# Latent-attention heads with moved gate tiles and the second rope half on GpSimd, and a second block with projection tiles on either side of the weighted sums

## The chip, the cores and the metric

One NeuronCore of a Trainium2 chip runs the whole forward pass of two blocks in one launch. The metric is the device time of that launch in microseconds (us). All engines run their own instruction streams, written out by hand, and meet in semaphores: TensorE (PE), VectorE (DVE), ScalarE (ACT), GpSimd (POOL) and the DMA queues, of which SP issues most.

## What is computed

Two blocks on a sequence of 512 positions of width 1024, in float32. The first has a pooling layer and a latent-attention layer (16 heads, 128 + 64 rope dimensions), the second a mixed layer of forgetting attention (8 heads of 64) and spatial gating, and a feed-forward. Cut to what the change touches:

```python
def mla_layer(x, cos, sin, norm_g, w_in, q_norm_g, w_q_b, kv_norm_g, w_kv_b, w_out):
    h = rmsnorm(x, norm_g)
    q_lat, kv_lat, k_rope, z = split(h @ w_in)            # z: the gates, 2048 wide
    q = (rmsnorm(q_lat, q_norm_g) @ w_q_b)                # per head 128 + 64
    kv = (rmsnorm(kv_lat, kv_norm_g) @ w_kv_b)            # per head k 128, v 128
    q_rope, k_rope = apply_rope(q_rope, cos, sin), apply_rope(k_rope, cos, sin)
    o = causal_mla_attention(q_nope, q_rope, k_nope, k_rope, v)
    return x + (o.reshape(B, S, MLA_WIDTH) * jax.nn.silu(z)) @ w_out

def second_block(x, ...):
    h = rms_norm(x, mix_norm_g) @ w_in                    # q, k, v, 8 gate logits, z
    log_f = jax.nn.log_sigmoid(f_logit + b_f)
    attn = forgetting_attention(q, k, v, log_f)
    sgu = spatial_gating(jax.nn.gelu(z), sgu_ln_g, sgu_ln_b, w_s, b_s)
    merged = concatenate([rms_norm(attn, out_norm_g[:D_ATTN]), rms_norm(sgu, out_norm_g[D_ATTN:])])
    x = x + merged @ w_out
    gate, up = split(rms_norm(x, ffn_norm_g) @ w_gate_up)
    return rms_norm(x + (silu(gate) * up) @ w_down, final_norm_g)
```

## The kernel before

Every float32 product is made of three passes with operands split in a high part (rounded to the matmul format) and the rest: high x high, high x low, low x high (`three`, L1347 to L1349). So each operand has a `_hi` and a `_lo` tensor; `_hi` is a copy by ScalarE, `_lo` a subtraction by VectorE or GpSimd.

The weights come as a stream of tiles of 128 x 1024 (512 KB). SP loads tile t into one of two `raw` buffers once the low part of tile t - 2 is made; ScalarE copies it into `w_hi` (L495, `split_tile`, three tiles ahead of its use), GpSimd subtracts into `w_lo` (L448), in a ring of four. TensorE waits for `tile_lo`, and sets `tile_used` at the tile's end. A whole tile is 24 matmuls of 512 columns (8 chunks x 3).

*Latent heads.* The projection `mla_in` makes five latent tiles, the key rope and 16 gate tiles z. Then heads come in four groups of four. For head h TensorE does: transposes of the probabilities for key blocks 0 and 1 (L1486, 7 matmuls), the scores of head h + 1 for query blocks 0 and 1 (L1347 to L1349, L1475, L1476), transposes for blocks 2 and 3 (3 matmuls), the scores for blocks 2 and 3, the weighted sum (`weigh_mla`), and then the units of the next group (`prepare`): keys, queries, two rope halves and values. The transposes of blocks 2 and 3 use the banks of blocks 0 and 1 again, so they wait until ScalarE (L655) and VectorE (L1101) have taken those out as `prob_t`. VectorE also takes the maxima (`peaks`, L1085), scales the probabilities (L1095), makes the low parts of the units (L995) and turns the rope queries: `turn_half` has two steps for half 0 (L1006, L1007) and four for half 1 (L1009 to L1014), `turned_low` two more; SP copies the turned rows into `rope_q` with 16 small DMAs a group (L391). The last group prepares nothing, so the last four heads stand directly one behind the other. The output product `mla_out` reads `y_hi` and `y_lo`, the latter made by GpSimd (L455).

*Second block.* Nine tiles `mix_qk` (four q, one with the 8 gate columns, four k), four `mix_v`, eight `mix_z`. Two z tiles are done ahead of the heads, one after each of the first six heads. A head's scores read `stacked`, into which SP copies its rows (L414, L416) while it also loads tiles. The layer norm of z's second half is on VectorE and GpSimd (L468, L470, L473). Then `sgu_mix`, the norms of both branches, and `mix_out`, in which one tile holds the weights of both branches for one output chunk; VectorE puts the two together in three steps for each chunk (L1290 to L1292), and the feed-forward's first tile starts with the last chunk of the norm (L867).

## Time and profile before

| | |
|---|---|
| time, median of 3 runs | 1397.96 us (1396.8 to 1399.28) |
| the profiled execution, own time | 1397.48 us |
| its span, first to last instruction | 1395.8 us |
| mean granted TensorE clock | 0.987 |
| busy: PE, DVE, ACT, POOL | 1340.8, 649.7, 538.4, 553.0 us |
| DMA | 135.42 MB, mean 97 GB/s |

The span is a little shorter than the time, which also holds what lies before and after the first and last instruction. A matmul's row ends later than the next one starts, since they are pipelined; starts are the better measure. The waits of an engine are sorted by the one it was released by.

### The profile page before, as it was taken

How to read it: one execution, taken by the hardware profiler on the slowest of the kernel's cores; microseconds unless marked ns; L12 is line 12 of the kernel's file. 1: busy time of each engine (PE TensorE's matmuls, PEld its weight loads, DVE VectorE, ACT ScalarE, POOL GpSimd, SP SyncE). 2: the span in 40 equal slices, each digit the busy share in tenths (PEclk: the TensorE clock that was granted, in tenths of full speed). 3: DMA queues.
4: the chain of work that ended last, by engine and by line, in shares of the span. 5: the costliest groups of instructions: out<-in, count | busy, mean ns of one | idle time of the engine just before them, and what ended most of it. 6: DMA issues, size and time to landing. Idle time of an engine off the chain costs nothing.

```text
span 1395.8 us, 16722 instructions
## 1 busy us (share of the span) xinstructions
PE 1340.8 (96%) x6170; PEld 1090.9 (78%) x6170; DVE 649.7 (47%) x1029; ACT 538.4 (39%) x893; POOL 553.0 (40%) x247
## 2 busy tenths in 40 slices
PE   7999999999999999999899999979899999999997
PEld 5888888887788777877788778877678888888886
DVE  7998547133643466565234853566642222221001
ACT  5233333233232555656533334664332322222112
POOL 4446444443353422214644443162344444444441
PEclk9999999999999999999999999998999999999999
DMA  4233322324132421322222346431222332222231
GB/s 154 88 106 119 99 91 91 106 91 150 61 121 69 143 61 46 98 54 76 91 91 97 114 151 160 107 113 55 82 91 90 96 100 90 90 95 86 92 102 64
DMA packets 40587, 135.42 MB, mean 97 GB/s; under 512 B 5936, under 2 KB 5936, under 8 KB 40016
## 3 DMA queue, kind: packets, MB, share of 16 engines
q1 hardware_dynamic: 38800, 126.18, 28.8%
q10 hardware_dynamic: 1728, 8.44, 1.6%
q8 instruction: 39, 0.64, 0.2%
q14 instruction: 20, 0.16, 0.0%
HBM read 117.76 MB, written 6.29 MB: 89 GB/s over the span
## 4 chain that ended last, share of the span: by engine, by line
PE 85%; DVE 5%; ACT 4%; issue 3%; POOL 1%; DMA 1%; SPq 0%; DVEq 0%; ACTq 0%; POOLq 0%
PE bank L1347 27%; PE bank L1349 27%; PE bank L1348 27%; PE bank L1486 1%; DVE prob_t L1101 1%; ACT f_prob L639 1%; PE bank L1476 1%; POOL w_lo L448 1%; PE bank L1475 1%; DVE pool_sqsum L877 1%; PE bank L1371 0%; DMA x<-x_in 0%; ACT w_hi L495 0%; DVE ffn_xg L867 0%; DVE y_out L1329 0%
## 5 line engine op out<-in xcount | busy, mean ns | idle before, releaser
L448 POOL TENSOR_TENSOR w_lo<-raw,w_hi 128x1024 fp32r<-128x1024 f32 x209 | 513.9, 2460 | 782.7 <-ACT w_hi L495 782.6
L495 ACT ACTIVATE w_hi<-raw 128x1024 fp32r<-128x1024 f32 x209 | 220.4, 1055 | 428.5 <-PE bank L1349 384.6
L1347 PE MATMUL bank<-ffn_xg,w_hi 128*128 128x512 f32 x352 | 141.0, 400 | 5.1 <-DVE ffn_xg L867 5.1
L1348 PE MATMUL bank<-ffn_xg,w_hi 128*128 128x512 f32 x352 | 140.2, 398 | 0.0
L1349 PE MATMUL bank<-ffn_xg,w_lo 128*128 128x512 f32 x352 | 140.2, 398 | 0.0
L1347 PE MATMUL bank<-pool_xg,w_hi 128*128 128x512 f32 x256 | 103.2, 403 | 9.2 <-DVE pool_xg L867 9.2
L1348 PE MATMUL bank<-pool_xg,w_hi 128*128 128x512 f32 x256 | 102.6, 401 | 0.0
L1349 PE MATMUL bank<-pool_xg,w_lo 128*128 128x512 f32 x256 | 102.5, 400 | 0.0
L1347 PE MATMUL bank<-y_hi,w_hi 128*128 128x512 f32 x256 | 101.5, 397 | 0.0
L1348 PE MATMUL bank<-y_lo,w_hi 128*128 128x512 f32 x256 | 101.5, 396 | 0.0
L1349 PE MATMUL bank<-y_hi,w_lo 128*128 128x512 f32 x256 | 101.5, 396 | 0.0
L1347 PEld LDWEIGHTS bank<-ffn_xg,w_hi 128*128 128x128 f32 x352 | 66.6, 189 | 22.8 <-DVE ffn_xg L867 6.5
L1349 PEld LDWEIGHTS bank<-ffn_xg,w_lo 128*128 128x128 f32 x352 | 66.7, 190 | 16.3
L1348 PEld LDWEIGHTS bank<-ffn_xg,w_hi 128*128 128x128 f32 x352 | 66.7, 190 | 16.2 <-issue 0.2
L892 DVE TENSOR_TENSOR x<-bank,x 128x512 f32<-128x512 f32 x16 | 11.1, 692 | 128.5 <-PE bank L1349 128.5
L1347 PE MATMUL bank<-w_hi,act 128*128 128x512 f32 x176 | 70.8, 403 | 0.0
L1347 PE MATMUL bank<-mla_xg,w_hi 128*128 128x512 f32 x176 | 70.6, 401 | 0.0
L1349 PE MATMUL bank<-mla_xg,w_lo 128*128 128x512 f32 x176 | 69.8, 396 | 0.0
L1348 PE MATMUL bank<-mla_xg,w_hi 128*128 128x512 f32 x176 | 69.8, 396 | 0.0
L1349 PE MATMUL bank<-w_hi,act 128*128 128x512 f32 x176 | 69.3, 394 | 0.0
L1348 PE MATMUL bank<-w_lo,act 128*128 128x512 f32 x176 | 69.0, 392 | 0.0
L1347 PEld LDWEIGHTS bank<-pool_xg,w_hi 128*128 128x128 f32 x256 | 48.9, 191 | 21.3 <-POOL w_lo L448 9.1
(327 smaller groups left out, 2815.8 us busy)
## 6 DMA issues: line engine op xcount, KB each, us to landing
raw<-stream SPq DMA_DIRECT2D x209, 512.0 KB, 3.4
spill<-x ACTq DMA_DIRECT2D x2, 2048.0 KB, 6.5
rope_q<-turned_hl SPq DMA_DIRECT2D x64, 64.0 KB, 2.5
stacked<-fq SPq DMA_DIRECT2D x24, 128.0 KB
stacked<-fk SPq DMA_DIRECT2D x24, 128.0 KB
x<-x_in SPq DMA_DIRECT2D x4, 512.0 KB, 6.6
x<-spill ACTq DMA_DIRECT2D x1, 2048.0 KB, 7.7
x<-spill SPq DMA_DIRECT2D x1, 2048.0 KB, 8.3
```

Source lines behind the costliest of these rows:

```text
L448: pool.tensor_tensor(w_lo[:, j % RING, :], raw[:, j % RAW, :], plain(w_hi[:, j % RING, :]), ALU.subtract).then_inc(tile_lo, 1)
L495: act.activation(w_hi[:, t % RING, :], raw[:, t % RAW, :], ACT.Copy).then_inc(tile_hi, 1)
L639: act.activation(target[:, ROW[b]:ROW[b + 1]], bank[SCORE_BANK[b]][:, SCORE_AT[b]:SCORE_AT[b] + n], ACT.Exp, bias=neg_peak[:, h % 2, b:b + ...
L877: dve.tensor_tensor(total, total, square(k), ALU.add).then_inc(n.summed, 1)
L892: dve.tensor_tensor(x[:, k, :], bank[(k + 4) % 8][:], x[:, k, :], ALU.add).then_inc(n.x_ready, 1)
L1101: dve.tensor_tensor(lo[:, COLUMN[b]:COLUMN[b + 1]], bank[3 + b % 2][:, 0:S - P * b], plain(hi[:, COLUMN[b]:COLUMN[b + 1]]), ALU.subtract). ...
L1347: pe.matmul(target, a_hi, b_hi, start=start, stop=False)
L1348: pe.matmul(target, a_hi, b_lo, start=False, stop=False)
L1349: return pe.matmul(target, a_lo, b_hi, start=False, stop=stop)
L1475: pe.matmul(target, rope_q[:, g % 2, j, a], rope_k_hi[:, 0:n], start=False, stop=False)
L1476: last = pe.matmul(target, rope_q[:, g % 2, j, a], rope_k_lo[:, 0:n], start=False, stop=True)
L1486: last = pe.transpose(bank[3 + b % 2][:, P * (q - b):P * (q - b + 1)], source[:, ROW[q] + P * b:ROW[q] + P * (b + 1)], ident[:])
```

## The change

In the latent layer:
- `TILE_SIZES`: the last 3 of the 16 gate tiles leave `mla_in` and become `mla_late`. The normalised input they need, `mla_xg_hi` and `mla_xg_lo`, is written to `xg_spill` by two DMAs of ScalarE's queue at the stage's start and read back by SP (`reload`, four DMAs into `zx`). TensorE does one late tile (`late_gate`) after each of heads 12, 13 and 14; ScalarE takes their silu there, and VectorE their evacuation.
- The scores of query block 2 move ahead of the second transposes. With the last head, where there are no scores, the first output tile stands in their place, four chunks at a time.
- For groups 1 to 3 ScalarE copies the bank of rope half 1 to `rope_2`, and GpSimd does its four steps and the two low parts (`turn_rows`).
- `y_lo` of chunks 8 to 15 goes from GpSimd to VectorE, after the last head. VectorE does `peaks` of bank 1 before the low parts of blocks 2 and 3.

In the second block:
- The gate tile goes; its 8 columns ride with the first z quarter, in two tiles of 1056 columns (`stream_wide`), whose four position blocks each have a bank of their own with 264 columns. The four transposes of the gates go with it.
- The tiles are in one list, `MIX`. Ahead of the heads: q0, k0, z0, z1, v0 to v3, q1, k1. The other ten stand in the heads, in `fill`: one part before the weighted sum and one after it. All scores of the next head come before the second transposes.
- `mix_out` has four tiles for the attention half and four for the gating half. `attn_product` is spread over heads 6 and 7, the gating and the norms; VectorE adds the attention half first (two steps a chunk, `add_attention`), then the gating half (one step). ScalarE, not VectorE, scales the gating branch. VectorE gates within the last head.
- The feed-forward starts with chunks 0 to 6 of its first two tiles, then chunk 7 of both (`first_tiles`).
- SP issues the stacking copies two or more tiles earlier for the last heads.

The diff, cut to its core:

```diff
-TILE_SIZES = (..., ("mla_in", LC + 1 + PC + 1),
-              ("heads", 5 * GROUPS - 1), ("mla_out", PC), ("mix_qk", 9), ("mix_v", 4), ("mix_z", 8),
+ZN = PC - 3
+TILE_SIZES = (..., ("mla_in", LC + 1 + ZN + 1),
+              ("heads", 5 * GROUPS - 1), ("mla_late", PC - ZN), ("mla_out", PC), ("mix", 20),
+MIX = (("q", 0), ("k", 0), ("z", 0), ("z", 1), ("v", 0), ("v", 1), ("v", 2), ("v", 3), ("q", 1), ("k", 1),
+       ("q", 2), ("k", 2), ("z", 2), ("z", 3), ("q", 3), ("k", 3), ("z", 4), ("z", 5), ("z", 6), ("z", 7))
...
 SP
+            sp.wait_ge(mla.scores, 3 * 12)
+            sp.wait_ge(zx_spilled, 32)
+            sp.wait_ge(rope_q_in, 256 * GROUPS)
+            for i in range(3):
+                reload(i)
+            load(0, TILE["heads"] + 5 * GROUPS + 1)
+            sp.wait_ge(tile_used, group_tile(GROUPS - 1, GH) + 1)
+            reload(3)
+            heads_after = {11: (0, 1), 13: (2, 3), 17: (4, 5), 19: (6,), 21: (7,)}
...
 POOL
+            def turn_rows(g):
+                pool.wait_ge(unit_evac, evacuated(("rope", g, 0)))
+                pool.wait_ge(rope_copied, g)
+                for i, (t, table, op) in enumerate(((turned_1, sin, ALU.subtract), (turned_2, cos, ALU.add))):
+                    pool.tensor_tensor(rope_t[:], rope_2[:], table[:], ALU.mult).then_inc(turn_steps, 1)
+                    pool.wait_ge(turn_steps, 2 * g - 1 + i)
+                    pool.tensor_tensor(t[:], t[:], rope_t[:], op).then_inc(turned, 1)
+                    pool.wait_ge(turned, 2 * g + i + 1)
+                for i, t in enumerate((turned_1, turned_2)):
+                    pool.wait_ge(turned_hi_done, 2 * g + i + 1)
+                    pool.tensor_tensor(turned_lo[:, i, :], t[:], plain(turned_hi[:, i, :]), ALU.subtract)...
...
 DVE, latent heads
                 if h + 1 < HEADS:
-                    peaks(mla, h + 1, MLA_SCALE, (0,))
+                    peaks(mla, h + 1, MLA_SCALE, (0, 1))
                 transposed_low(mla, h, prob_t_hi, prob_t_lo, (2, 3))
...
+            for k in range(8, PC):
+                dve.wait_ge(y_hi_done, PC + k + 1)
+                dve.tensor_tensor(y_lo[:, k, :], z[:, k, :], plain(y_hi[:, k, :]), ALU.subtract).then_inc(y_last_done, 1)
...
 PE, latent heads
-                for blocks in ((0, 1), (2, 3)):
+                for blocks, behind in (((0, 1), (0, 1, 2)), ((2, 3), (3,))):
                     transposes(mla, h, prob, probs, NB * (h + 1), blocks)
                     if h + 1 < HEADS:
-                        scores_mla(h + 1, blocks)
+                        scores_mla(h + 1, behind)
+                    else:
+                        pe.wait_ge(mla_evac, LC + 1 + ZN + 2)
+                        out_tile("mla_out", 0, PC, range(4) if blocks[0] == 0 else range(4, 8))
                 weigh_mla(h)
                 if g < GROUPS:
                     prepare(g, j)
+                elif h < HEADS - 1:
+                    late_gate(h - 12)
...
 PE, second block
+            def fill(h, part):
+                if h == 0:
+                    qk_tile(4 + part)
+                elif h == 2:
+                    pe.wait_ge(z_evac, NB + 2 * part + 2)
+                    qk_tile(6 + part)
+                elif h in (1, 3):
+                    sgu_tile(h + 1 + part)
+                elif h < 6:
+                    sgu_tile(h + 2, range(2 * part, 2 * part + 2))
+                elif h == 6 and part == 0:
+                    attn_product(0, (0, 1))
+                    attn_product(1, (0, 1))
             for h in range(FOX_HEADS):
+                transposes(fox, h, f_prob, probs, NB * (HEADS + h + 1), (0, 1))
+                if h + 1 < FOX_HEADS:
+                    scores_fox(h + 1, (0, 1, 2))
+                else:
+                    attn_product(0, (2,))
+                    attn_product(1, (2,))
+                    pe.wait_ge(ws_lo_done, 1)
+                    pe.wait_ge(zvn_lo_done, NB)
+                    sgu_mix(range(6))
+                transposes(fox, h, f_prob, probs, NB * (HEADS + h + 1), (2, 3))
+                fill(h, 0)
+                if h == FOX_HEADS - 1:
+                    sgu_mix((6, 7))
                 weigh_fox(h)
+                fill(h, 1)
...
 DVE, output of the second block
+            def add_attention(chunks):
+                for k in chunks:
+                    wait_half(0, k)
+                    t = mixed[:, k % 2, :]
+                    settle(dve.tensor_tensor(t, bank[ATTN_BANK[k]][:], attn_inv[:], ALU.mult))
+                    dve.tensor_tensor(x[:, k, :], t, x[:, k, :], ALU.add).then_inc(attn_added, 1)
+            add_attention(range(4))
             for c in range(SC):
+                if c == 2:
+                    add_attention((4,))
                 dve.wait_ge(sgu_hi_done, c + 1)
                 dve.scalar_tensor_tensor(sgu_lo[:, c, :], ...)
+            add_attention(range(5, DC))
...
```

How the instructions stand on the engines at three places. First TensorE in the second block, from the first transposes of a head to what follows its second transposes (`ident,f_prob` are transposes, `stacked` scores, `f_prob_t,fv` the weighted sum); before:

```order
L1486 MATMUL bank<-ident,f_prob 128x128 x7
L1613 MATMUL bank<-stacked 128x128
L1614 MATMUL bank<-stacked 128x128
L1613 MATMUL bank<-stacked 128x256
L1614 MATMUL bank<-stacked 128x256
L1486 MATMUL bank<-ident,f_prob 128x128 x3
L1613 MATMUL bank<-stacked 128x384
L1614 MATMUL bank<-stacked 128x384
L1613 MATMUL bank<-stacked 128x512
L1614 MATMUL bank<-stacked 128x512
L1347 MATMUL bank<-f_prob_t,fv 128x512
```

and the same place, head 0, in the changed kernel:

```order
L1638 MATMUL bank<-ident,f_prob 128x128 x7
L1783 MATMUL bank<-stacked 128x128
L1784 MATMUL bank<-stacked 128x128
L1783 MATMUL bank<-stacked 128x256
L1784 MATMUL bank<-stacked 128x256
L1783 MATMUL bank<-stacked 128x384
L1784 MATMUL bank<-stacked 128x384
L1783 MATMUL bank<-stacked 128x512
L1784 MATMUL bank<-stacked 128x512
L1638 MATMUL bank<-ident,f_prob 128x128 x3
L1490 MATMUL bank<-mix_xg,w_hi 128x512
```

The four longer score matmuls moved ahead of the second transposes, and a projection tile (24 matmuls, the first is shown) stands between them and the weighted sum.

Second, VectorE after the first head of a group (`turned` and `rope_t` are the rope queries, `k` a unit's low part, `prob_t` the transposed probabilities of the next head); before:

```order
L1125 TENSOR_TENSOR z<-bank,z 128x512
L995 TENSOR_TENSOR k<-bank,k 128x512
L1006 TENSOR_TENSOR turned<-bank,cos 128x512
L1007 TENSOR_TENSOR turned<-bank,sin 128x512
L1009 TENSOR_TENSOR rope_t<-bank,sin 128x512
L1010 TENSOR_TENSOR turned<-turned,rope_t 128x512
L1012 TENSOR_TENSOR rope_t<-bank,cos 128x512
L1014 TENSOR_TENSOR turned<-turned,rope_t 128x512
L1101 TENSOR_TENSOR prob_t<-bank,prob_t 128x512
```

and in the changed kernel:

```order
L1232 TENSOR_TENSOR z<-bank,z 128x512
L1098 TENSOR_TENSOR k<-bank,k 128x512
L1109 TENSOR_TENSOR turned<-bank,cos 128x512
L1110 TENSOR_TENSOR turned<-bank,sin 128x512
L1204 TENSOR_TENSOR prob_t<-bank,prob_t 128x512
```

Four steps left VectorE there. They are on GpSimd now, between weight tiles (`w_lo`), third place:

```order
L504 TENSOR_TENSOR rope_t<-rope,sin 128x512
L506 TENSOR_TENSOR turned<-turned,rope_t 128x512
L504 TENSOR_TENSOR rope_t<-rope,cos 128x512
L506 TENSOR_TENSOR turned<-turned,rope_t 128x512
L510 TENSOR_TENSOR turned_hl<-turned,turned_hl 128x512 x2
L496 TENSOR_TENSOR w_lo<-raw,w_hi 128x1024 x5
```

Before, GpSimd had nothing but `w_lo` in the heads; now six steps come in each of three groups, and the next weight tile of its stream stands behind them.

## Rows read from the trace of the kernel before

**Rows 1.** The page: its head, TensorE's line, the granted clock of 40 slices.
```profile
span 1395.8 us, 16722 instructions
...
PE 1340.8 (96%) x6170; PEld 1090.9 (78%) x6170; DVE 649.7 (47%) x1029; ACT 538.4 (39%) x893; POOL 553.0 (40%) x247
...
PEclk9999999999999999999999999998999999999999
```

**Rows 2.** Waits of TensorE: released by; us in total, times, longest.
```profile
PE bank L1486 <- DVE prob_t L1101: 11.5, 16, 2.0
...
PE bank L1486 <- DVE f_prob_t L1101: 8.2, 7, 2.0
PE bank L1347 <- DVE ffn_xg L867: 5.1, 2, 3.4
PE bank L1613 <- DMA stacked<-c_parts: 3.6, 1, 3.6
PE bank L1486 <- DVE prob L1095: 2.7, 3, 0.9
PE bank L1347 <- DVE x L1292: 2.0, 1, 2.0
PE bank L1347 <- DVE zu L1225: 1.7, 1, 1.7
```

**Rows 3.** Windows: length; busy PE, PEld, DVE, ACT, POOL; clock; DMA share, GB/s.
```profile
540.00:620.00 80.00, 75.96 (x387) 63.37 (x387) 51.17 (x129) 44.19 (x103) 16.80 (x7) 0.96 0.18 52
920.00:1020.00 100.00, 83.70 (x376) 67.96 (x375) 65.77 (x98) 46.07 (x83) 41.81 (x23) 0.88 0.28 93
```

**Rows 4.** Timeline of TensorE in `mla_in`: start, duration, instruction.
```profile
459.77 0.40 PE L1348 MATMUL bank<-mla_xg,w_hi 128*128 128x512 f32 x1
...
460.94 0.40 PE L1347 MATMUL bank<-lat,w_hi 128*128 128x512 f32 x1
```

**Rows 5.** Timeline of TensorE, first head of a group; in brackets idle before, releaser.
```profile
551.24 0.28 PE L1475 MATMUL bank<-rope_k,rope_q 128*128 128x256 f32 x1
551.36 0.28 PE L1476 MATMUL bank<-rope_k,rope_q 128*128 128x256 f32 x1
553.38 0.70 PE L1486 MATMUL bank<-ident,prob 128*128 128x128 f32 x3 [1.74 <-DVE prob_t L1101]
```

**Rows 6.** Timeline of VectorE at the same place.
```profile
552.55 1.15 DVE L1101 TENSOR_TENSOR prob_t<-bank,prob_t 128x512 fp32r<-128x512 f32 x2
```

**Rows 7.** Timeline of TensorE in a head of the second block.
```profile
884.49 0.70 PE L1486 MATMUL bank<-ident,f_prob 128*128 128x128 f32 x3 [0.78 <-DVE f_prob_t L1101]
```

**Rows 8.** Groups by line: busy us, mean ns; idle before, releaser.
```profile
L448 POOL TENSOR_TENSOR w_lo<-raw,w_hi 128x1024 fp32r<-128x1024 f32 x209 | 513.9, 2460 | 782.7 <-ACT w_hi L495 782.6
L455 POOL TENSOR_TENSOR y_lo<-z,y_hi 128x512 fp32r<-128x512 f32 x16 | 20.1, 1292 | 6.6 <-ACT y_hi L554 6.6
L495 ACT ACTIVATE w_hi<-raw 128x1024 fp32r<-128x1024 f32 x209 | 220.4, 1055 | 428.5 <-PE bank L1349 384.6 <-DMA raw<-stream 41.5 <-DVE mix_sqsum L877 2.3
```

**Rows 9.** DMA issues: KB each, us to landing; and one row of SP's timeline.
```profile
raw<-stream SPq DMA_DIRECT2D x209, 512.0 KB, 3.4
...
x<-spill SPq DMA_DIRECT2D x1, 2048.0 KB, 8.3
...
615.45 4.95 SPq L391 DMA_DIRECT2D rope_q<-turned_hl  x8
```

**Rows 10.** VectorE beside GpSimd: timeline rows, and the line's least, median and most ns.
```profile
901.01 0.88 DVE L1095 TENSOR_SCALAR f_prob<-f_prob,inv_sum 128x128 f32<-128x128 f32 x3
...
922.47 4.21 DVE L1095 TENSOR_SCALAR f_prob<-f_prob,inv_sum 128x128 f32<-128x128 f32 x3
...
972.67 2.60 DVE L1292 TENSOR_TENSOR x<-mixed,x 128x512 f32<-128x512 f32 x1
...
972.32 2.40 POOL L448 TENSOR_TENSOR w_lo<-raw,w_hi 128x1024 fp32r<-128x1024 f32 x1 [19.52 <-ACT w_hi L495]
...
L1292 DVE TENSOR_TENSOR x<-mixed,x x8: 691/2020/2691, 972.7 to 1014.6; 128x512 f32<-128x512 f32 x8
```

748 lines of the change are left out of this document (442 added, 306 removed).

## The prediction

> **What bounds the kernel now.** I read the page first, then the list of waits of TensorE, then windows, then single places of the timeline. The page shows TensorE busy for 96% of the span of 1395.8 us and its clock granted at nine tenths or more in all but one of 40 slices [rows 1]. So only two things can bring time: matmuls that go, and moments in which TensorE stands still or runs at half clock. The list of waits gives the second by cause [rows 2]. In the sixteen latent heads it is the second group of transposes behind VectorE's `prob_t` (11.5 us in 16 waits) and the first group behind `prob` (2.7 in 3). In the second block it is the same for `f_prob_t` (8.2 in 7), the copies into `stacked` (3.6), the first products of the feed-forward (5.1), the output product (2.0) and the gating (1.7). Everything ahead of the heads is not touched.
>
> A listed wait is a little short of what it costs. Two score matmuls start 0.12 us apart (551.24, 551.36), the transposes start at 553.38, 2.02 later, and the list calls 1.74 of that idle [rows 5]: the modelled tail hides 2.02 - 0.12 - 1.74 = 0.16 us of each wait. The granted clock is 0.96 over 80 us of the heads and 0.88 over the 100 us around the end of the second block's attention and its output product [rows 3]; full clock there would be worth at most 0.04 x 80 = 3.2 and 0.12 x 100 = 12 us. TensorE is busy 83.7 of those 100 us, so I count 10. In both windows the lowered level (1.2 instead of 2.4 GHz) comes with the idle places.
>
> **The change, part by part.**
>
> *The gate tile.* The ninth query/key tile, which held eight useful columns, goes: 8 chunks x 3 matmuls of 512 columns. Five such steps take 460.94 - 459.77 = 1.17 us, 0.234 each [rows 4]: 24 x 0.234 = 5.6 us, and nothing waits there, so it is all on the path. The four small transposes of the gates go too (0.3). The gates now ride as 8 more columns on two z tiles: 96 matmuls x 8 columns at 0.234/512 us a column = 0.35. Net **-5.6**.
>
> *The latent heads.* Between the two groups of transposes TensorE has now three score blocks instead of two; the third is 5 matmuls of 384 columns, 5 x 384 x 0.234/512 = 0.88 us. The waits there average 11.5/16 = 0.72, and most are shorter than 0.88. The first head of a group waits 1.74 because VectorE does the four steps of the second rope half first and reaches `prob_t` only at 552.55 [rows 5, 6]; these four, and the two low parts, go to GpSimd, with ScalarE copying the bank. The last four heads have no preparation to hide behind; three gate tiles of the first projection (3 x 5.6 us) come behind them, moved, not added, so they cost nothing in themselves and cover the 2.7 and the last four `prob_t` waits. Gain: 11.5 + 2.7 + 19 x 0.16 = 17.2, plus the clock's 3.2: 20.4.
> What it costs. (a) `y_lo` 8 to 15 now stand on VectorE behind the last head: the second output tile waits for z (0.68) and the first `y_lo` (0.69) and may meet GpSimd once (below); bounds 0.7 and 4, I take 2. (b) GpSimd's turn is four steps, then two low parts, at 1.29 each for this size [rows 8], with ScalarE's high parts between, which it reaches only in the next head: the low part is ready about as late as before, but the heads until then are shorter by their waits, and SP's 16 copies take twice 4.95 us with a tile load between [rows 9]. I get the last copy landing within half a microsecond of the scores that need it: 0 to 2 us in each of three groups, I take 1 in all. (c) Spilling and reloading the normalised input, 4 MB each way: a reload of 2 MB landed after 8.3 us [rows 9], so the 3.5 MB that stand ahead of one tile load on SP's queue take about 14.5; by the program that tile's split comes some 16 us after the reload may start and the landing some 17.5: 1 us, bounds 0 and 6. The spill has three tiles of lead (16 us) and costs nothing. Net **-16.4**.
>
> *The second block.* Projection tiles stand now before and after each weighted sum, and all score blocks before the second transposes. In the head at 882 the transposes wait 0.78 us, 0.94 with the hidden part [rows 7], with four score matmuls as cover; the other four (two of 384 and two of 512 columns) add 1792 x 0.234/512 = 0.82. With the third transpose, which waits once more for VectorE, I leave 0.35 us a head of the 8.2. The copies for the last head are issued two tiles earlier, so the 3.6 goes. The output product is cut into an attention half, which fills the gating and the norm's root, and a half that needs only one addition per chunk; the feed-forward does seven chunks of two tiles (14 x 3 x 0.234 = 9.8 us) before it needs the last chunk: 5.1 + 2.0 go. With the gating, 8.2 + 3.6 + 5.1 + 2.0 + 1.7 = 20.6, tails 12 x 0.16 = 1.9, clock 10: 32.5.
> What it costs: transposes 7 x 0.35 = 2.5; `prob` of the first head needs the fourth projection evacuated first, 0.7; the layer norm's chain on GpSimd (four blocks of two steps of 1.29, three weight tiles of 2.46, then four low parts of 1.29 [rows 8]: 12 x 1.29 + 3 x 2.46 = 23 us) against 22 us of TensorE work up to the gating's matmuls, and ScalarE held for its input before head 6: 0 to 9, I take 4.5; the last head's gating 1.5; the output product waiting for the normed branch behind the additions, 0 to 6, I take 2.5; one half-clock stretch that stays, 1.7. Together 13.4, net **-19.1**.
>
> Where GpSimd and VectorE meet decides (a) and the last block. At 972 VectorE's addition of two SBUF operands takes 2.60 us and ends with GpSimd's 2.40 us weight step, and the eight of its line range from 0.69 to 2.69; the three scalings of `f_prob`, 0.88 us together at 901, take 4.21 at 922 while GpSimd works on the layer norm [rows 10]. The Trainium skill, "SBUF — State Buffer", section "Who interferes with whom", says that a VectorE instruction with two SBUF inputs, or in a two-port mode, and a GpSimd instruction exclude each other for their whole length. By that rule the trace agrees, and the change puts more on both sides: 18 steps on GpSimd, 8 `y_lo` and 8 additions on VectorE.
>
> **Sum.** -5.6 - 16.4 - 19.1 = -41.1. The profiled execution took 1397.48 us (span 1395.8), within 0.5 us of the median of 1397.96. 1397.5 - 41.1 = **1356.4 us**.
>
> **Rivals.**
> 1. *Nearly all waits go.* The costs above are at their lower ends: of 58.5 us gained (5.6 + 20.4 + 32.5) only the transposes' 1.5, `y_lo` 0.7 and a clock stretch 1.7 stay. 1397.5 - 54.6 = 1343. For it: the fillers are 2.8 to 5.6 us long where the waits are 1 to 2. Against: the chains of the layer norm and the output product are not shortened. Chance 0.17.
> 2. *VectorE and GpSimd hold each other.* Each of the 16 two-operand steps moved onto or kept on VectorE meets a GpSimd step and takes 2.6 instead of 0.69 (+1.9) [rows 10], half of them in front of TensorE: 8 x 1.9 = 15. 1371. For it: 2.0 us is the median of those eight steps now. Against: in the heads VectorE has 3.5 to 5.6 us behind its last scaling. This is the case that the cited section would foretell. Chance 0.17.
> 3. *Slower: the weight ring runs dry.* Each of the eight heads of the second block asks for two tiles; if ScalarE reaches their splits only behind its exponentials, load 3.4 [rows 9], split 1.06 and GpSimd's 2.46 [rows 8] stand open in front of TensorE in each: 6.9 x 8 = 55 us against 41 gained: 1411. It decides from 41/8 = 5.1 us a head. For it: two raw buffers, and SP's queue holds the stacking waits between loads. Against: the ring is three tiles ahead (5.6 us each). Chance 0.03.
> 4. *The late gate tiles do not fill:* the change does not do there what it says. Their input lands late or the head-side copies hold the queue, and head 12 waits for it, 8 us more than the 1 taken: 1364. Chance 0.05.
>
> **Numbers.** The forecast has 0.58, its own range 1347 to 1365. The range to hold the time 8 times in 10 takes in the nearer parts of rivals 1 and 2 and all of 4: 1339 to 1373. A difference under 0.2% (2.8 us) could not be told from none. Faster 0.96, same 0.01, slower 0.03.
>
> **What would show it.** Right: about 24 + 4 fewer matmuls; the waits for `prob_t` and `f_prob_t` under 4 us together instead of 19.7; none for `ffn_xg`; clock 0.98 or more over the 100 us before the feed-forward; the heads from first scores to output product 3 x 5.6 - 16 us longer than before, that is about equal. Left over: waits for `zvn_lo`/`prob_t` at heads 6 and 7 of the second block, for `y_lo` once, for `sgu_lo`. Wrong: waits for w_lo on TensorE's weight loads (rival 3), for `zx` (rival 4), `y_lo`, additions and scalings on VectorE at 2 us and more with TensorE behind them (rival 2), or half-clock stretches as many as before.

## The result and the profile after

The changed kernel takes **1349.01 us** (median of 4 runs, 1346.8 to 1349.57) against 1398.62 for the kernel before in the same job: ratio 0.9637, 95% interval 0.961 to 0.9664. Forecast were 1356.4 us, with the range 1339 to 1373. The profiled execution has a span of 1347.8 us, 48.0 less than that of before. One execution of the kernel before, in the last job, took 2186.01 us at a mean granted clock of 0.557 and is left out of every comparison.

The head of the page, TensorE's line and its clock answer to [rows 1]:

```profile
span 1347.8 us, 16621 instructions
...
PE 1316.0 (98%) x6142; PEld 1075.7 (80%) x6142; DVE 647.5 (48%) x1014; ACT 540.0 (40%) x903; POOL 564.1 (42%) x256
...
PEclk9999999999999999999999999999999999999999
```

There are 28 matmuls fewer, and TensorE is busy for 98% of the span. The list of its waits answers to [rows 2]:

```profile
PE bank L1490 <- DVE pool_xg L970: 9.3, 1, 9.3
PE bank L1638 <- DVE f_prob_t L1204: 3.6, 2, 2.7
PE bank L1490 <- DVE y_lo L1243: 2.9, 2, 1.5
PE bank L1490 <- DVE attn L1326: 1.9, 1, 1.9
PE bank L1490 <- DVE v L1098: 1.8, 1, 1.8
...
PE bank L1862 <- DVE sgu L1425: 0.9, 1, 0.9
PE bank L1638 <- DVE mean_sq L1271: 0.8, 1, 0.8
PE bank L1638 <- DVE f_prob L1198: 0.5, 1, 0.5
```

All 16 waits for `prob_t` are gone, of those for `f_prob_t` two of seven are left, and `stacked` and `ffn_xg` don't appear. New are `y_lo`, `attn`, `v` and `mean_sq`. The wait at the very start (`pool_xg`, 9.3) was there before. Two windows of the changed kernel, columns as in [rows 3]: 80 us of heads at the same place of the work as there, and the last 100 us before the feed-forward:

```profile
521.70:601.70 80.00, 79.90 (x445) 68.69 (x444) 50.20 (x137) 49.41 (x118) 34.51 (x20) 1.00 0.28 86
866.00:966.00 100.00, 93.02 (x525) 79.53 (x525) 79.68 (x132) 62.14 (x119) 46.32 (x25) 0.97 0.33 106
```

The second window of [rows 3] reaches 14 us into the feed-forward. The last 100 us before it are, in the trace of before:

```profile
905.00:1005.00 100.00, 87.17 (x445) 73.65 (x444) 63.53 (x118) 51.04 (x100) 40.02 (x22) 0.91 0.25 82
```

The granted clock is 1.00 instead of 0.96 in the heads, 0.97 instead of 0.91 ahead of the feed-forward.

Where the 48.0 us went, by the first start of each stage in the two traces:

| from, to | before | after | difference | predicted |
|---|---|---|---|---|
| start, first `mla_in` matmul (no edit there) | 328.2 | 327.2 | -1.0 | 0 |
| first `mla_in` matmul, first scores | 147.0 | 129.7 | -17.3 | -16.8, moved |
| first scores, first `mix` matmul | 292.1 | 291.4 | -0.7 | +16.8 - 16.4 |
| first `mix`, first feed-forward matmul | 238.4 | 217.8 | -20.6 | } -5.6 - 19.1 |
| first feed-forward, first down projection | 256.2 | 247.7 | -8.4 | } |
| the rest | 134.0 | 134.0 | 0 | 0 |
| sum | 1395.8 | 1347.8 | -48.0 | -41.1 |

The latent part gave 18.0 for 16.4, the second block 29.0 for 24.7, and 1.0 us came from a stretch in which nothing was edited.

### The profile page after: what moved, and what is told of

The parts are those of the page before. It is cut to its first block, busy times and chain, and to the rows that moved or that the text cites. A ratio compares the mean times of both kernels' runs of the same rounds, so it can differ in the third digit from the quotient of the medians.

```text
span 1347.8 us, 16621 instructions
## 1 busy us (share of the span) xinstructions
PE 1316.0 (98%) x6142; PEld 1075.7 (80%) x6142; DVE 647.5 (48%) x1014; ACT 540.0 (40%) x903; POOL 564.1 (42%) x256
## 4 chain that ended last, share of the span: by engine, by line
PE 91%; DVE 4%; ACT 2%; DMA 1%; POOL 1%; issue 0%; DVEq 0%; SPq 0%; ACTq 0%
PE bank L1490 29%; PE bank L1492 29%; PE bank L1491 29%; PE bank L1638 2%; DMA raw<-stream 1%; PE bank L1627 1%; PE bank L1628 1%; DVE pool_xg L970 1%; PE bank L1514 1%; DVE x L1418 1%; DVE y_lo L1243 0%; DVE pool_sqsum L980 0%; DMA x<-x_in 0%; DVE y_out L1472 0%; POOL w_lo L496 0%
## 5 line engine op out<-in xcount | busy, mean ns | idle before, releaser
L496 POOL TENSOR_TENSOR w_lo<-raw,w_hi 128x1024 fp32r<-128x1024 f32 (+1 forms) x208 | 513.3, 2470 | 730.3 <-ACT w_hi L566 730.3
L566 ACT ACTIVATE w_hi<-raw 128x1024 fp32r<-128x1024 f32 (+1 forms) x208 | 218.4, 1054 | 385.7 <-PE bank L1492 322.9
L1490 PE MATMUL bank<-mla_xg,w_hi 128*128 128x512 f32 x152 | 60.9, 400 | 0.0
L1491 PE MATMUL bank<-mla_xg,w_hi 128*128 128x512 f32 x152 | 60.1, 396 | 0.0
L1492 PE MATMUL bank<-mla_xg,w_lo 128*128 128x512 f32 x152 | 60.1, 395 | 0.0
```

Source lines behind the costliest of these rows:

```text
L496: pool.tensor_tensor(w_lo[:, j % RING, 0:width], raw[:, j % RAW, 0:width], plain(w_hi[:, j % RING, 0:width]), ALU.subtract).then_inc(tile_ ...
L566: act.activation(w_hi[:, t % RING, 0:width], raw[:, t % RAW, 0:width], ACT.Copy).then_inc(tile_hi, 1)
L1490: pe.matmul(target, a_hi, b_hi, start=start, stop=False)
L1491: pe.matmul(target, a_hi, b_lo, start=False, stop=False)
L1492: return pe.matmul(target, a_lo, b_hi, start=False, stop=stop)
```

## Three places where TensorE still waits

**The transposes of head 6 of the second block.** TensorE, then ScalarE, from the timelines of the changed kernel:

```profile
899.87 0.39 PE L1784 MATMUL bank<-stacked 68*128 68x512 f32 x1
902.93 0.30 PE L1638 MATMUL bank<-ident,f_prob 128*128 128x128 f32 x1 [2.67 <-DVE f_prob_t L1204]
...
898.44 1.06 ACT L566 ACTIVATE w_hi<-raw 128x1024 fp32r<-128x1024 f32 x1 [4.20 <-DMA raw<-stream]
899.41 2.17 ACT L881 ACTIVATE zvn_hi<-zv 128x512 fp32r<-128x512 f32 x4
901.49 0.95 ACT L738 ACTIVATE f_prob_t<-bank 128x512 fp32r<-128x512 f32 x2
```

The list names VectorE, which only came last: ScalarE waited 4.2 us for a weight tile, and did the four `zvn_hi` before it took out the transposed probabilities.

The list of the weight loads' waits has one row that the matmuls' list does not show. The first of its two waits is the one at the start, the second ends at 913.21, in front of the products on `attn`; VectorE's step beside it:

```profile
PEld bank L1490 <- POOL w_lo L496: 11.4, 2, 9.3
...
910.25 2.84 DVE L1326 SCALAR_TENSOR_TENSOR attn<-attn,cols 128x512 fp32r<-128x512 f32 x1
```

GpSimd makes the four `zvn_lo` first and the weight tile's low part from 910.08 to 912.55. VectorE's `attn` takes 2.84 us beside it and ends at 913.10; the same step takes 0.75 where GpSimd does nothing. TensorE waits 2.1 us for the two.

**The last chunks of `y_lo`.** TensorE, then VectorE:

```profile
660.69 0.27 PE L1492 MATMUL bank<-prob_t,v 128*128 128x128 f32 x1
662.44 0.47 PE L1490 MATMUL bank<-y_hi,w_hi 128*128 128x512 f32 x1 [1.47 <-DVE y_lo L1243]
...
666.94 0.50 PE L1490 MATMUL bank<-y_hi,w_hi 128*128 128x512 f32 x1 [1.47 <-DVE y_lo L1243]
...
661.00 0.69 DVE L1232 TENSOR_TENSOR z<-bank,z 128x512 f32<-128x512 f32 x1 [3.73 <-PE bank L1492]
661.61 6.48 DVE L1243 TENSOR_TENSOR y_lo<-z,y_hi 128x512 fp32r<-128x512 f32 x7
```

VectorE stood idle for 3.7 us and then began with all of them at once. Seven take 6.48 us, 0.93 each instead of 0.69; a GpSimd weight step runs from 663.55 on. Two waits follow, 1.69 and 1.63 us by starts.

**The values of the last group.** TensorE, SP and ScalarE:

```profile
613.80 0.50 PE L1490 MATMUL bank<-w_hi,lat 128*128 128x512 f32 x1 [1.77 <-DVE v L1098]
...
597.83 1.29 SPq L430 DMA_DIRECT2D zx<-xg_spill  x3
599.79 0.33 SPq L413 DMA_DIRECT2D raw<-stream  x1
...
611.47 1.06 ACT L566 ACTIVATE w_hi<-raw 128x1024 fp32r<-128x1024 f32 x1 [1.89 <-DMA raw<-stream]
612.44 1.07 ACT L651 ACTIVATE v<-bank 128x512 fp32r<-128x512 f32 x2
```

This is the price of the reload: the tile load behind it was issued at 599.79 and landed only at 611.45, 11.7 us later, where the median load takes 3.4. ScalarE waits for it with the copies of `v` behind. A half-clock stretch of 3.4 us follows the wait, at 614.2.

## Experiments: parts undone

All but the last are the changed kernel with one part put back. The first four ran in one job; the two on the scores of the second block and on the feed-forward ran in a later one, without the changed kernel beside them. They are compared with the changed kernel's repeat, 1348.87 us (1346.81 to 1350.66); the kernel before took 1396.95 us in the first of these jobs and 1398.52 in the second.

**The same kernel again.**

> The changed kernel once more, as the base for the others of this call. Expected: 1347 to 1350 us. Its trace also tests whether the matmuls' own step is a property of the kernel: in the unchanged first 328 us, 512-column matmuls start 0.2343 us apart on average in the trace of before and 0.2335 in that of the changed kernel. Theory A (it belongs to the kernel): 0.2335 again. Rival B (it belongs to the chip or the hour): anything else.

1348.87 us, and the step of the matmuls is 0.2333 us. Theory A so far; the section on the ring goes on from here.

**Scores of query block 2 behind the second transposes again.**

```diff
-                for blocks, behind in (((0, 1), (0, 1, 2)), ((2, 3), (3,))):
+                for blocks, behind in (((0, 1), (0, 1)), ((2, 3), (2, 3))):
```

> Latent heads only: the scores of query block 2 go back behind the second transposes, and the maxima with them; all else as in the changed kernel. Theory A (the third score block is what covers VectorE's prob_t): each of 15 heads loses 0.88 us of cover; the average wait of before was 0.72 + 0.16 hidden, of which the heads that had the rope steps in front held about 1 us more each in 3 places: 15 x 0.88 - 3 = about 10 us longer, 1359, with 12 or more waits for prob_t in the list. Rival B (the rope steps and the late tiles took the waits away, the third block is spare): 0 to 3 us longer, waits in none or few of the heads.

1354.92 us (1354.38 to 1356.46), **6.1 longer**, between the two. The row of its list of waits:

```profile
PE bank L1638 <- DVE prob_t L1204: 1.9, 10, 0.2
```

By starts, 15 heads lose 0.25 to 0.36 us at the second transposes, 4.8 in all. The three transposes then also take longer: 0.47 us from the first of them to the next matmul instead of 0.25. From its first transposes to its weighted sum a head takes 4.74 to 4.84 us, 4.28 with the changed order, 7.9 us over 15 heads; the half-clock stretch at 614, which this execution does not have, and a shorter wait for `v` give part of it back. So the waits come back in every head, but each is about a third of the 0.88 that I had put in.

**The second rope half on VectorE again.**

```diff
-                    pool.tensor_tensor(rope_t[:], rope_2[:], table[:], ALU.mult).then_inc(turn_steps, 1)
+                    dve.tensor_tensor(rope_t[:], rope_2[:], table[:], ALU.mult).then_inc(turn_steps, 1)
...
-                    pool.tensor_tensor(t[:], t[:], rope_t[:], op).then_inc(turned, 1)
+                    dve.tensor_tensor(t[:], t[:], rope_t[:], op).then_inc(turned, 1)
```

> The four steps on the second rope half go back from GpSimd to VectorE (reading the same SBUF copy that ScalarE makes; the two low parts stay on GpSimd). Three groups. Theory A (they delayed prob_t; the longer score cover takes 0.88 of it): the 1.74 us wait of before comes back as about 0.9 + 0.16 in each of three heads, 3 us longer, 1352. Rival B (VectorE has room for them behind the longer cover): within 1 us of the changed kernel. Rival C (with two SBUF operands they now exclude GpSimd's weight steps and take 2.6 us instead of 0.7): up to 3 x 4 x 1.9 = 23 us of VectorE time, 8 to 15 us longer, and w_lo late.

1354.68 us (1354.28 to 1355.66), **5.8 longer**. Its wait row, and VectorE at the second of the three places:

```profile
PE bank L1638 <- DVE prob_t L1197: 5.1, 3, 1.7
...
529.58 0.69 DVE L1208 TENSOR_TENSOR rope_t<-rope,sin 128x512 f32<-128x512 f32 x1 [1.38 <-ACT rope L654]
530.30 0.69 DVE L1210 TENSOR_TENSOR turned<-turned,rope_t 128x512 f32<-128x512 f32 x1
531.03 0.69 DVE L1208 TENSOR_TENSOR rope_t<-rope,cos 128x512 f32<-128x512 f32 x1
531.76 0.69 DVE L1210 TENSOR_TENSOR turned<-turned,rope_t 128x512 f32<-128x512 f32 x1
532.49 1.16 DVE L1197 TENSOR_TENSOR prob_t<-bank,prob_t 128x512 fp32r<-128x512 f32 x2
```

Three waits of 1.7, 1.85 each by starts: theory A's mechanism, but nearly twice its size. The size is not that of the old arrangement, since VectorE now idles 1.38 us for ScalarE's copy of the bank, where it waited 0.68 for TensorE when it read the bank itself. With the old steps and the longer cover 1.02 are left in each place (the last run of this section), close to theory A's 0.9 + 0.16. So the longer cover alone does not free these three places; with the move to GpSimd they are free. Rival C did not come, but this run does not test it: all twelve steps take 0.69, and GpSimd has no instruction in any of the three stretches. The same trace has a step of this kind ahead of the heads, at 428.20, that meets GpSimd's weight step (427.22 to 429.70), and that one takes 2.06.

**All filling work behind the weighted sum.**

```diff
-                fill(h, 0)
                 if h == FOX_HEADS - 1:
                     sgu_mix((6, 7))
                 weigh_fox(h)
+                fill(h, 0)
                 fill(h, 1)
```

> Second block: the part of the filling tiles that stands between the second transposes and the weighted sum goes behind the weighted sum, next to the other part; the work and its amount stay. Theory A (the place on either side is what hides the evacuation of the second transposes): the weighted sum waits for ScalarE's and VectorE's two steps, about 1.8 us in each of 7 heads, 12.6, and TensorE's pauses bring half-clock stretches of 3.4 us back (1.7 us each, 2 to 4 of them): 14 to 19 us longer, 1363 to 1368. Rival B (only the total of filling work between two heads counts, since the probabilities of the next head are the long chain): 0 to 4 us longer.

1349.44 us (1347.31 to 1351.06), 0.6 longer, less than these runs can tell apart, and inside **rival B**'s 0 to 4 us. TensorE in the second head, with not one idle mark:

```profile
830.50 0.70 PE L1638 MATMUL bank<-ident,f_prob 128*128 128x128 f32 x3
830.97 0.47 PE L1490 MATMUL bank<-f_prob_t,fv 128*128 128x512 f32 x1
...
831.74 0.34 PE L1490 MATMUL bank<-f_prob_t,fv 128*128 128x384 f32 x1
...
832.39 0.39 PE L1490 MATMUL bank<-f_prob_t,fv 128*128 128x256 f32 x1
```

The weighted sum begins with the two key blocks taken out long before; its six matmuls on them cover the evacuation of the third. In the ordinary heads what the title calls filling on either side is worth nothing as a place. In the last head it is worth something: with the attention product behind the weighted sum of head 6, the wait for `f_prob` is 2.1 us instead of 0.5, 1.5 more by starts. That only the amount between two heads counts, the other half of rival B, was not tried: no run changed the amount.

**The longer scores behind the second transposes of the second block.**

```diff
-                    scores_fox(h + 1, (0, 1, 2))
+                    scores_fox(h + 1, (0,))
...
                 transposes(fox, h, f_prob, probs, NB * (HEADS + h + 1), (2, 3))
+                if h + 1 < FOX_HEADS:
+                    scores_fox(h + 1, (1, 2))
```

> Second block: only the shortest scores (blocks 0 and 1) stand between the two groups of transposes, the longer ones behind, as before; the filling tiles stay. Theory A (the four longer score matmuls are what covers f_prob_t): in before the six ordinary heads lost 0.9 to 1.5 us each here and the first 1.8; they come back: 7 heads, 6 to 8 us longer, 1355 to 1357, with some 7 waits for f_prob_t. Rival B (VectorE and ScalarE are less loaded at this place now, so that the waits went by themselves): 0 to 3 us longer.

1351.82 us (1349.99 to 1353.06), **3.0 longer** than the changed kernel in the job before. The waits are as theory A has them, one in each head, while the time is at rival B's edge:

```profile
PE bank L1638 <- DVE f_prob_t L1204: 7.6, 7, 2.8
```

By starts four ordinary heads lose 0.94 us each, exactly as such a head in the trace of before, against 0.11 to 0.12 with the changed order, and the first head 0.87 against 0.05: 4.1 us more. The losses of the other two (about 1.1 and 2.9) are there in both. So in these five heads the cover is what removed them, and the lighter load of the engines had no part in it. Theory A's 6 to 8 us took seven heads to be of this kind. That the time moved by less than 4.1 goes with the clock: this execution has no half-clock stretch in the second block, the changed kernel has two.

**The feed-forward's first two tiles one after the other.**

```diff
-                for chunks in (range(DC - 1), (DC - 1,)):
+                for chunks in ((range(DC),)):
                     for j in range(2):
```

> The feed-forward does its first tile whole, then its second, as before; all else as in the changed kernel. Theory A (the seven chunks of two tiles cover the last chunk's norm): a wait of 3 to 5 us for ffn_xg comes back and one half-clock stretch (1.7): 3 to 7 us longer. Rival B (the output product now hands out its chunks evenly, one addition each, so that the norm keeps up): 0 to 1.5 us longer.

1347.55 us (1346.68 to 1348.29), 1.3 shorter if anything, and `ffn_xg` is not in the list of waits: **rival B**. So the 5.1 us of [rows 2] did not go because seven chunks of two tiles come first. That they went because the output product now leaves one addition per chunk behind it fits, but was not tried by itself.

**One part alone, in the kernel before.**

```diff
-                for blocks in ((0, 1), (2, 3)):
+                for blocks, behind in (((0, 1), (0, 1, 2)), ((2, 3), (3,))):
...
-                        scores_mla(h + 1, blocks)
+                        scores_mla(h + 1, behind)
```

> The kernel before with one part of the change alone: in the latent heads the scores of query block 2 stand between the two groups of transposes (and VectorE takes their maximum ahead of the second low parts). Worked out by starts from the trace of before: 9 or 10 ordinary heads lose 0.35 us, three first heads of a group 1.9, the last heads 1.1 each. Theory A (0.88 us more cover takes what it can of each): 10 x 0.35 + 3 x 0.88 + 3 x 0.88 = 8.8 us, of which some comes back as in the reverse run, which gave 6.1: 6 to 9 us shorter, 1389 to 1392. Rival B (in the heads with rope steps VectorE only gets to the maxima and so to the next probabilities later, and a wait on prob takes its place): 3 us or less.

1385.88 us (1383.17 to 1386.71), ratio 0.9907 (0.9869 to 0.9944): **12.8 shorter**, more than either theory, though the interval reaches down to 7.8. The rows of its waits:

```profile
PE bank L1486 <- DVE prob_t L1101: 5.0, 5, 1.2
...
PE bank L1486 <- DVE prob L1095: 2.9, 3, 1.0
```

From the first scores to the first `mix` matmul its trace has 279.9 us; the trace of before and its repeat both have 292.1. The 12.2 us can be laid out by the stretch from a head's first transposes to its weighted sum. The ten ordinary heads take 4.28 us instead of 4.85, 5.7 together: 0.35 of the 0.57 is the wait and 0.22 are the three transposes themselves, which no list of waits shows. The three first heads of a group take 5.52 instead of 6.41 and twice 7.45, 4.8 together. In the two long ones lies part of the clock's gain: the trace of before has half-clock stretches of 3.4 us at 554.7 and 609.3, just behind their waits, and this one has neither. The last heads give 1.7 together, although a new stretch stands at 660.9.

Done alone the part gives 12.8, undone it costs 6.1: the late tiles and GpSimd's turn cover the same places and the same clock. Gains of parts of this change do not add up.

Executions of one kernel differ mostly by their time at half clock. That time can be taken out: a run with the mean granted clock m lost at most (1 - m) x its span to it. The means of the runs without this loss (standard errors 0.1 to 0.6 us):

| kernel | runs | mean without the loss | difference | difference of medians |
|---|---|---|---|---|
| the changed kernel, repeated | 4 | 1342.7 | | |
| scores of block 2 split again | 4 | 1349.8 | +7.0 | +6.1 |
| second rope half on VectorE | 4 | 1349.1 | +6.3 | +5.8 |
| filling behind | 4 | 1343.9 | +1.2 | +0.6 |
| scores of the second block split | 4 | 1346.6 | +3.9 | +3.0 |
| feed-forward one by one | 4 | 1342.5 | -0.3 | -1.3 |
| before, in the job of the long cover | 13 | 1381.4 | | |
| before, with the long cover | 4 | 1371.2 | -10.1 | -12.8 |

## Experiments: why untouched matmuls became shorter

From 10 to 328 us the two kernels run the same matmuls in the same order. Neighbouring 512-column matmuls start 0.2342 us apart on average before and 0.2333 after, counted alike in all traces; the expectations give 0.2343 and 0.2335 for the same two. Nothing in my prediction has a place for it. One thing that differs there is the weight ring: `raw`, `w_hi` and `w_lo` have rows of 1056 columns instead of 1024, for the two wide tiles.

> The kernel before, profiled once more. In the unchanged first 328 us its 512-column matmuls started 0.2343 us apart; in the changed kernel and three variants of it 0.2333 to 0.2335. Theory A (the step belongs to the kernel): 0.2343 again, and about 4.5 us of the 49 come from it. Rival B (it belongs to the execution or the chip): 0.2333 to 0.2335 here too, and a span of about 1391 us instead of 1395.8.

1398.23 us (1395.56 to 1403.61), step 0.2341: it belongs to the kernel.

```diff
-        raw = sb("raw", [P, RAW, 1024])
-        w_hi = sb("w_hi", [P, RING, 1024], f32r)
-        w_lo = sb("w_lo", [P, RING, 1024], f32r)
+        raw = sb("raw", [P, RAW, 1056])
+        w_hi = sb("w_hi", [P, RING, 1056], f32r)
+        w_lo = sb("w_lo", [P, RING, 1056], f32r)
```

> The kernel before, with nothing changed but the row length of the weight ring: 1056 columns for raw, w_hi and w_lo as in the changed kernel, of which 1024 are used (the rope tables move by 1.5 KB to make room). Both profiles of before show 512-column matmuls 0.2343 and 0.2341 us apart in the first 328 us, all seven of the changed kernel and its variants 0.2333 to 0.2335. Theory A (the layout of the ring in memory does it): 0.2333 to 0.2335 here, and 4 to 5 us shorter than before, about 1393. Rival B (it comes from the program's own length or order, or from elsewhere): 0.2341 to 0.2343, and the time of before, 1396 to 1399.

The step is 0.2333, theory A. The time is 1396.88 us (1395.33 to 1401.67), ratio 0.9989 (0.9972 to 1.0006), 1.8 us by the medians: not the 4 to 5 us. Was it the row length or only the shifted addresses of everything above the ring?

```diff
         w_lo = sb("w_lo", [P, RING, 1024], f32r)
+        unused = sb("unused", [P, 320])
```

> The kernel before with the weight ring as it was (rows of 1024 columns), but 1.25 KB left free behind it, so that everything above lies at the addresses that it has with the wide ring (the rope tables too). With the wide ring the 512-column matmuls of the first 328 us started 0.2333 us apart, without it 0.2341 and 0.2343. Theory A (the ring's own row length does it): 0.2341 to 0.2343 here. Rival B (the place of the other tensors does it): 0.2333. The time should be that of before in either case, 1396 to 1399, since the wide ring's 0.0009 us a matmul was given back in half-clock stretches.

1397.98 us (1393.81 to 1401.72), step 0.2341: theory A, the row length of the ring. With the row length the places of `w_hi` and `w_lo` themselves and of their four tiles change too; which of these it is was not separated. The first pass of `mla_in` in four traces (least, median and most ns; first and last start), of before, with the wide ring, with the shift alone, and of the changed kernel:

```profile
L1347 PE MATMUL bank<-mla_xg,w_hi x176: 392/397/798, 328.2 to 460.2; 128*128 128x512 f32 x176
```

```profile
L1347 PE MATMUL bank<-mla_xg,w_hi x176: 391/394/795, 327.2 to 458.8; 128*128 128x512 f32 x176
```

```profile
L1348 PE MATMUL bank<-mla_xg,w_hi x176: 392/397/798, 328.2 to 460.2; 128*128 128x512 f32 x176
```

```profile
L1490 PE MATMUL bank<-mla_xg,w_hi x152: 391/394/795, 327.2 to 442.0; 128*128 128x512 f32 x152
```

The wide ring is 1.0 us ahead at 328 and 1.4 at 460. Its profiled execution then lost that, with a mean granted clock of 0.984 against 0.987. At equal clock the gain shows: the three runs of it at 0.987 took 1396.70 to 1396.98 us, the three of before at 0.987 in the same job 1399.20 to 1400.08, about 3 us more. With the loss at half clock taken out as above, all its ten runs have a mean of 1378.4 us against 1381.4 for the thirteen of before, 3.0 less; the shifted kernel and its before both have 1380.7. Why the wide ring's ten runs have a slightly lower clock (0.9863 on average, before 0.9875) stays open.

The traces also show which matmuls gain. Where a ring tile is the stationary operand, the one that the weight load brings into TensorE (the products with `mla_xg`, `y_hi`, `ffn_xg` and others), the 512-column step falls from 0.2343 to 0.2335 us. Where it is the moving one, in the down projection (`w_hi,act`), the step is 0.2334 before and 0.2335 with the wide ring, and the stretch from the first down projection to the end is 134.0 and 134.1 us.

## Experiments: moves at the waits that were left

The five moves, as the expectation lists them; the second and the third as code (the `zvn_hi` of head 5 stand in head 6):

```diff
                 transposed_high(fox, h, f_prob_t_hi, (2, 3))
+                if h == 6:
+                    for b in range(NB):
+                        act.wait_ge(zvn_ready, b + 1)
+                        act.activation(zvn_hi[:, b, :], zv[:, b, :], ACT.Copy).then_inc(zvn_hi_done, 1)
...
-                    attn_product(0, (2,))
-                    attn_product(1, (2,))
                     pe.wait_ge(ws_lo_done, 1)
                     pe.wait_ge(zvn_lo_done, NB)
                     sgu_mix(range(6))
+                    attn_product(0, (2,))
+                    attn_product(1, (2,))
```

> The changed kernel with five moves at the places where its trace still shows TensorE waiting; the same work. (1) y_lo of chunks 8 to 11 before VectorE waits for the last head's output: the two waits for y_lo, 3.3 us by starts. (2) ScalarE makes the four zvn_hi behind the next head's transposed copies, not in front of them: most of the 2.8 us at 900. (3) sgu_mix stands before the attention product of pair 2 in the last head: the 2.0 us at 911. (4) ScalarE scales all four blocks of f_prob for heads 6 and 7, where VectorE's three took 4.4 and 3.3 us beside GpSimd: 0.8 us at 910. (5) In the last group ScalarE splits its weight tile behind the v units' copies: 1.9 us at 612. If each place is really the last to end there: 3.3 + 2.2 + 2.0 + 0.6 + 1.7 = 9.8 us shorter, 1339. Rival (behind each wait another stands by, the layer norm's chain on GpSimd above all): 5 us or less, with a wait for zvn_lo in the last head.

**1341.02 us** (1340.52 to 1341.28), ratio to before 0.9579 (0.9551 to 0.9607), 7.9 shorter than the changed kernel's repeat, for 9.8 expected and 5 or less by the rival. About half of it is the clock's: without the loss at half clock the mean is 1338.6, 4.1 shorter. The waits for `y_lo`, `v` and `attn` are gone. What is left or took their place:

```profile
PE bank L1643 <- ACT f_prob L730: 2.4, 1, 2.4
PE bank L1643 <- DVE f_prob_t L1204: 1.8, 2, 1.0
```

ScalarE's `zvn_hi` had only moved in front of the exponentials of the last head. Two further moves answer that:

```diff
                 transposed_high(fox, h, f_prob_t_hi, (0, 1))
+                if h == 6:
+                    split_mix(22)
...
+                if h == 5:
+                    for b in range(NB - 1):
+                        act.wait_ge(zvn_ready, b + 1)
+                        act.activation(zvn_hi[:, b, :], zv[:, b, :], ACT.Copy).then_inc(zvn_hi_done, 1)
-                for i in ((12, 13), (14, 15), (16, 17), (18, 19), (20, 21), (22,), (23,), ())[h]:
+                for i in ((12, 13), (14, 15), (16, 17), (18, 19), (20, 21), (), (23,), ())[h]:
...
-                for i in ((20,), (21, 22), (23,))[step]:
+                for i in ((20,), (21,), (22, 23))[step]:
```

> The five moves, of which the second left a wait of 2.4 us for the probabilities of the last head (ScalarE made four zvn_hi in front of its exponentials), with two more: ScalarE makes zvn_hi of blocks 0 to 2 in the stretch in which it waited 3.1 us for a weight tile, and splits that tile behind the next head's first transposed copies; GpSimd makes zvn_lo one weight tile earlier. Theory A (the chain is ScalarE's order alone): the 2.4 us and 0.7 of the 1.05 at 894 go, 3 us shorter than the five moves, 1338. Rival B (the layer norm's chain on GpSimd is as late: zvn_lo ended at 904.0 and TensorE would want it at 902): the wait turns into one for zvn_lo, 1 us or less is gained, 1340 to 1341.

**1339.88 us** (1339.76 to 1340.29), 1.1 shorter still. TensorE at the place:

```profile
901.40 0.98 PE L1649 MATMUL bank<-ident,f_prob 128*128 128x128 f32 x7 [0.97 <-ACT f_prob L730]
904.92 0.47 PE L1501 MATMUL bank<-attn,w_hi 128*128 128x512 f32 x1 [0.38 <-DVE attn L1337]
907.49 0.70 PE L1649 MATMUL bank<-ident,f_prob 128*128 128x128 f32 x3 [0.93 <-DVE f_prob_t L1210]
```

The 2.4 became 0.97, and 0.38 and 0.93 stand behind it where the five moves had none and 0.2: rival B's size, though not its wait, since `zvn_lo` is not among them. The 1.1 us are the clock's: this execution has no half-clock stretch ahead of the last 4 us, that of the five moves has one at 902.6, and without the loss at half clock both have a mean of 1338.6. This version beats both kernels, by 9.1 us against the changed kernel's first median and by 58.8 against the median of before in its job.

## Why the prediction was right, and where it was not

The sum was -41.1, measured are -48.0. Of the difference about 3 us are the ring's row length, a term that the prediction did not have, and some 4 are costs priced too high.

*The gate tile, -5.6.* Right as far as a trace shows it: 28 matmuls fewer, and no wait where the eight columns now ride.

*Latent heads, -16.4; 18.0 came.* The step that failed is "the waits there average 11.5/16 = 0.72". An average hid three kinds: by starts ten ordinary heads lost 0.35, the three first heads of a group 1.9, the last ones 1.1 to 2.2 with their `prob` waits. It also left out what no wait shows, 0.22 us in the transposes of each ordinary head. The part's sum could not bring this to light, since it takes the total of the list and not the share of a head. So the third score block was more than enough for the ten and not enough for the three, which the rope's move freed (5.8 undone); that the two together end the waits was right. The clock's term was 3.2 and came as the difference of two half-clock stretches to one, 1.7. (a) `y_lo`, taken as 2 with bounds 0.7 and 4: 3.3 by starts. (b) `rope_q`, 1: right in its size. In one of the three groups the last copy lands at 549.14 and the scores that need it start at 549.23, 0.3 us late; in the repeat, whose row is below, it is 0.8, and in the other groups under 0.1. (c) the reload, 1 with bounds 0 and 6: nothing at `zx`; the tile behind it was late as said, and that shows as 1.9 at `v`, whose copies stand behind the tile's split on ScalarE. That place I had not named, nor the half-clock stretch that follows it.

```profile
549.64 0.30 PE L1490 MATMUL bank<-k,q 128*128 128x128 f32 x1 [0.56 <-issue]
```

*The second block, -19.1; 23.4 came beside the gate tile.* By starts, the gaps above 0.3 us between matmuls there gave 17.2 of it (27.2 in 19 places before, 10.0 in 9 after). The other 6.2 are the clock outside these gaps, the ring, and gaps below 0.3 us, which I have not separated. The clock as a whole is worth at most 8.5 (23.9 us at half clock before, 6.8 after), against 10 - 1.7 forecast; the ring about 1, an estimate from the 1.0 us that it gives in the first 328. Two reasons in it were wrong with the sum near: "the feed-forward does seven chunks of two tiles before it needs the last chunk: 5.1 go" names the wrong part (undone, nothing returned), and the tiles on either side of the weighted sum have no effect as places. Right were the scores as cover (0.82 forecast, 0.83 a head measured), the stacking copies (no wait), `prob` of the first head (0.7 forecast, 0.94), and the chain of the layer norm, 4.5 with bounds 0 and 9: the head of 902.93 loses 2.8 and the next places 0.8 and 2.0, 5.6.

The time lies inside the forecast's own range (1347 to 1365), but near its end: *rival 1* (1343) was off by 6.0, the forecast by 7.4. The five moves show what kept the kernel from rival 1. *Rival 2* holds as a mechanism but not as a price. VectorE, then GpSimd, in the changed kernel:

```profile
893.51 4.43 DVE L1198 TENSOR_SCALAR f_prob<-f_prob,inv_sum 128x128 f32<-128x128 f32 x3
...
892.69 2.41 POOL L496 TENSOR_TENSOR w_lo<-raw,w_hi 128x1024 fp32r<-128x1024 f32 x1
895.05 1.30 POOL L536 TENSOR_TENSOR zv<-zv,ln_g 128x512 f32<-128x512 f32 x1
896.43 1.29 POOL L538 TENSOR_TENSOR zv<-zv,ln_b 128x512 f32<-128x512 f32 x1
```

The three scalings take 4.43 us beside GpSimd, as the 4.21 of [rows 10]; free of it they take 0.88. The same at 907.07 with 3.26. The Trainium skill, "SBUF — State Buffer", section "Who interferes with whom", has a VectorE instruction in a two-port mode, which a `tensor_scalar` like this one can enter, and a GpSimd instruction exclude each other for their whole length, and these rows agree. But TensorE lost 0.1 us at the first and 0.54 us at the second, since other products stood in front. There are two places where TensorE did stand behind such a pair: the seven `y_lo` that took 6.48 us where 0.69 each would be 4.8, with a wait of 1.6 behind them, and `attn` at 910.25, 2.84 us instead of 0.75, where GpSimd's own weight tile was late as well. Together they are some 3 us, not the 15 of rival 2. One reading in the prediction is off: the addition at 972.67 does not end with GpSimd's step (974.72) but 0.55 us behind it (975.27), as if most of its own work stood behind. *Rival 3* (the ring dry) did not come in the heads as it foresaw, but its sign did once: the weight loads wait 2.1 us for `w_lo` at 913.21, behind GpSimd's `zvn_lo`. *Rival 4* (late tiles that don't fill) did not come: `zx` is not in the list.

Of the signs named, the clock was to be 0.98 or more over the last 100 us before the feed-forward; it was 0.97 (0.91 before). Of the signs of being wrong, the one of rival 3 came once. The others held: 28 matmuls, 3.6 us of waits for `prob_t` and `f_prob_t` together, none for `ffn_xg`, heads and output product together as long as before with 16.8 us more work in them.

## What to carry to other kernels

Sort the waits of one releaser by size before you price their cover: ten of 0.35 and three of 1.9 need different cures, and an average of 0.72 prices neither. What covers a wait is work between the same two points: the longer scores between the two groups of transposes did it, and the filling before or behind the weighted sum made no difference to an ordinary head. Two covers of one place don't add up, so a part's worth undone (6.1) is not its worth alone (12.8). When a wait is named after the last engine in a chain, look one engine further back for an instruction in the wrong order: five moves of order, one of them from VectorE to ScalarE, gave another 7.9 us without less work, about half of it through the clock.

## What the runs showed of the hardware

- The row length of the weight ring in SBUF changes the matmuls' own step: 0.2341 to 0.2342 us for 512 columns with rows of 1024 float32 columns, 0.2333 to 0.2334 with 1056, over the first 328 us (fourteen traces without exception: four of the first kind; the changed kernel, its repeat, its seven variants and the wide ring in the kernel before of the second). It does so only where the ring holds the stationary operand. Moving the other tensors by the same 1.25 KB does nothing. It is 0.4%, and 1.0 us in the first 328. Why the row length matters was not tried further.
- Less idle time on TensorE went with more granted clock and less spread. The kernel before ran from 1392.59 us at a mean clock of 0.992 to 1403.61 at 0.983, the changed one from 1346.8 to 1350.66 at 0.995 to 0.996, the seven moves from 1339.76 to 1340.29, all four at 0.999. In the trace of before each of the seven half-clock stretches ahead of the end begins within a wait of TensorE of 1.9 us or more, or at most 1.4 us behind one. Not every such wait is followed by one: of the three at first heads of a group, 1.9 each, those ending at 553.4 and 608.0 are, the one ending at 500.3 is not. So a wait removed here can pay twice.
- A VectorE step with two SBUF operands took 2.1 to 2.8 us where it met a GpSimd weight step and 0.69 to 0.75 where GpSimd did nothing (`turned` at 428.20 in the run with the rope half on VectorE, `attn` at 910.25 in the changed kernel). The step just ahead of the first of these reads one operand from a PSUM bank (`rope_t<-bank,cos`, 427.48), and took 0.69 beside the same GpSimd step.
